# Four attention heads one projection tile earlier, and two residual scalings in other places

## The reference

```python
for l in range(DEPTH):                      # DEPTH = 2
    h = rmsnorm_2(x, attn_norm[l])
    proj = jnp.einsum('bsd,de->bse', h, w_in[l])          # 1024 -> 3072
    sb_q, sb_k, sb_v, df_q, df_k, df_v = jnp.split(proj, splits, axis=-1)
    sb_out = stick_breaking_attention(...)                # 8 heads of 64
    dq, dk = rope(df_q ...), rope(df_k ...)               # 4 heads, two maps of 64 each
    df_heads = differential_attention(dq, dk, dvv, lam)   # softmax(map 0) - lam * softmax(map 1)
    df_out = rmsnorm_2(df_heads, subln_norm[l]) * (1.0 - lambda_init)
    x = x + jnp.einsum('bse,ed->bsd', mixed, w_o[l])
    h = rmsnorm_2(x, mlp_norm[l])
    u = jnp.square(jax.nn.relu(h @ w_ff1[l]))
    x = x + u @ w_ff2[l]
```

## Time and profile before

| | us |
|---|---|
| median of 3 runs | 1552.63 (1552.49 to 1553.12) |
| profiled execution | 1552.31 |
| its span | 1550.6 |
| TensorE busy | 1528.4 |
| VectorE busy | 1060.4 |
| ScalarE busy | 820.0 |

### The profile page before, as it was taken

How to read it: one execution, slowest core, us unless ns; L and a number is a source line. 1 busy time by engine, 2 the same in 40 slices (tenths; PEclk the granted TensorE clock), 3 DMA queues, 4 the chain that set the end, 5 groups by cost and what they waited for, 6 DMA issues and landing times.

```text
span 1550.6 us, 23427 instructions
## 1 busy us (share of the span) xinstructions
PE 1528.4 (99%) x8755; PEld 1292.1 (83%) x8755; DVE 1060.4 (68%) x1774; ACT 820.0 (53%) x1399; POOL 181.4 (12%) x146
## 2 busy tenths in 40 slices
PE   8999999999999999999999999999999999999998
PEld 7777888777788778898989888888788898989886
DVE  6886557566876876875858555775885885848653
ACT  5556533555655864645445335664874645545332
POOL 4001222032000213010100011000223010100001
PEclk9999999999999999999999999999999999999999
DMA  5211232322221113332332323212112233232331
GB/s 179 74 56 55 82 95 96 109 96 82 82 80 58 55 55 96 109 104 87 103 99 98 109 82 109 82 55 82 55 55 82 91 101 109 83 108 90 100 109 55
DMA packets 127300, 135.83 MB, mean 88 GB/s; under 512 B 2458, under 2 KB 120804, under 8 KB 127204
## 3 DMA queue, kind: packets, MB, share of 16 engines
q1 hardware_dynamic: 126048, 133.18, 26.9%
q0 software_dynamic: 288, 1.05, 0.2%
q10 hardware_dynamic: 868, 0.31, 0.1%
HBM read 132.43 MB, written 2.10 MB: 87 GB/s over the span
## 4 chain that ended last, share of the span: by engine, by line
PE 89%; DVE 3%; issue 3%; ACT 2%; POOL 1%; DVEq 0%; POOLq 0%; ACTq 0%
PE U L1942 19%; PE U L1944 19%; PE U L1943 19%; PE Z L2250 3%; PE Z L2251 3%; PE Z L2249 3%; PE U L1987 2%; PE U L1989 2%; PE U L1988 2%; PE U L2251 1%; PE U L2249 1%; PE U L2250 1%; PE Z L2124 1%; PE O L2176 1%; PE Z L2139 1%
## 5 line engine op out<-in xcount | busy, mean ns | idle before, releaser
L1942 PE MATMUL U<-MH,WL 128*128 128x512 f32 x848 | 337.2, 398 | 1.9 <-DVE tb L1610 1.7
L1944 PE MATMUL U<-MH,WH 128*128 128x512 f32 x848 | 331.1, 390 | 0.0
L1943 PE MATMUL U<-ML,WH 128*128 128x512 f32 x848 | 330.8, 390 | 0.0
L1132 DVE TENSOR_TENSOR WL<-raw,WH 128x1024 fp32r<-128x1024 f32 x181 | 234.6, 1296 | 81.6 <-ACT WH L643 71.9
L1942 PE MATMUL U<-XH,WL 128*128 128x512 f32 x592 | 237.3, 401 | 2.2 <-DVE WL L1455 1.1
L1944 PE MATMUL U<-XH,WH 128*128 128x512 f32 x592 | 231.4, 391 | 0.0
L1943 PE MATMUL U<-XL,WH 128*128 128x512 f32 x592 | 231.1, 390 | 0.0
L643 ACT ACTIVATE WH<-raw 128x1024 fp32r<-128x1024 f32 x197 | 205.7, 1048 | 19.1 <-PE Z L2251 16.7
L1942 PEld LDWEIGHTS U<-MH,WL 128*128 128x128 f32 x848 | 159.4, 188 | 43.2 <-issue 8.4
L1944 PEld LDWEIGHTS U<-MH,WH 128*128 128x128 f32 x848 | 159.3, 188 | 33.8
L1943 PEld LDWEIGHTS U<-ML,WH 128*128 128x128 f32 x848 | 159.6, 188 | 31.6 <-issue 0.7
(11 more groups left out here) (303 smaller groups left out, 3059.6 us busy)
## 6 DMA issues: line engine op xcount, KB each, us to landing
raw<-in_w_ff SPq DMA_DIRECT2D x64, 1024.0 KB, 5.4
raw<-in_w_in SPq DMA_DIRECT2D x24, 1024.0 KB, 5.1
raw<-in_attn_w_in SPq DMA_DIRECT2D x9, 1024.0 KB, 5.2
raw<-in_pool_w_in SPq DMA_DIRECT2D x8, 1024.0 KB, 5.5
raw<-in_w_o SPq DMA_DIRECT2D x8, 1024.0 KB, 5.1
raw<-in_attn_w_out SPq DMA_DIRECT2D x4, 1024.0 KB, 5.1
raw<-in_pool_w_out SPq DMA_DIRECT2D x4, 1024.0 KB, 5.2
xin<-in_x SPq DMA_DIRECT2D x2, 1024.0 KB, 6.5
```

Of the source, the lines that this page charges most:

```text
L1132: v.tensor_tensor(w_slot(WL, t, shape), src, w_slot(WH, t, shape).bitcast(F32), ALU.subtract).then_inc(lo_done, 1)
L1942: mm(o, wl, xh, start=first, stop=False, **kw)
L1943: mm(o, wh, xl, start=False, stop=False, **kw)
L1944: return mm(o, wh, xh, start=False, stop=last, **kw)
```

## The change

The head's first tile becomes 4+3d instead of 5+3d, and with it every step of a differential head comes one tile earlier in both layers. The scores of heads 0 and 2 then stand two tiles behind their query tile (tiles 4 and 10, queries in 2 and 8) instead of three. The third residual scaling of layer 0 moves from tile 4 to tile 6, the fourth from tile 7 to tile 9. VectorE's ordinary tile gains the branch for `df_f`, because head 3's last transpose now falls in tile 17 instead of 18. No instruction is added or removed on any engine.

```diff
--- before.py
+++ after.py
@@ -95,7 +95,7 @@
             return step
 
         for d in range(4):
-            first = 4 * (5 + 3 * d)
+            first = 4 * (4 + 3 * d)
             for i, when in enumerate((0, 2, 2)):
                 at(first + when, op="df_qk", d=d, i=i)
             for i in range(3):
@@ -1409,8 +1409,8 @@
                 if value_tile:
                     take(s, 0, l)
                     conv(s["t"] + 2)
-                if l == 0 and at in (2, 3, 4):
-                    residual((0, 2, 4)[at - 2])
+                if l == 0 and at in (2, 3):
+                    residual((0, 2)[at - 2])
                 for st in df_t:
                     if st["i"] == 1 and not (value_tile and before["kind"] in ("dfk", "dfq")):
                         df_evict(st)
@@ -1419,8 +1419,10 @@
                     df_norm(st, l)
                 for st in steps_of(s, "sb_o"):
                     sb_low(st)
-                if l == 0 and at == 7:
-                    residual(6)
+                for st in steps_of(s, "df_f"):
+                    df_low(st, l)
+                if l == 0 and at in (6, 9):
+                    residual(4 if at == 6 else 6)
 
             df_mix = {l: {i + 1: st["d"] for i, x in enumerate(plan["layer", l]) for st in x["steps"] if st["op"] == "df_qk" and st["i"] == 2}
                       for l in range(DEPTH)}
```

## The result

| | before | after |
|---|---|---|
| median, us | 1552.57 (1552.49 to 1553.12, 4 runs) | 1573.53 (1572.20 to 1573.96, 4 runs) |
| profiled execution, us | 1552.31 | 1573.96 |
| span, us | 1550.6 | 1572.2 |
| TensorE busy, us | 1528.4 | 1538.3 |
| granted clock, mean | 0.999 | 0.994 |

The ratio is 1.0134, interval 1.0122 to 1.0146: 21.0 us slower, where 13.8 were forecast and the range ended at 1571.5. The direction and every forecast wait of 0.7 us or more came. The prediction failed on one step, TensorE's clock.

What follows compares the result with a forecast made beforehand. TensorE, busy 1528.4 of 1550.6 us, was taken as the bound, so new waits add time. Terms of 6.75 (layer 0) and 7.05 (layer 1) give 13.8 on 1552.3: 1566.1, median 1566.4, range 1561.5 to 1571.5.

Steps and rivals of the forecast that it cites:

- Scores of head 0: Tile 4: TensorE waits for VectorE's add of tile 2's rotated query, +1.9 us in layer 0, +2.2 in layer 1.
- Head 0's combination, tile 6: VectorE's combination in tile 5 delays its value take, so TensorE starts tile 6 late, +0.7 us in each layer.
- Tiles 10 to 12: Late normalization and value takes put tile 12 at S+15.4 (S: start of head's second score round), +2.4 us each layer.
- Head 1's turns: Tile 9: ScalarE evicts turn 0 behind shifts waiting for the previous rotation; turn 1 late, +2.2 us in each layer.
- Head 2 and 3: Tiles 13 to 17: nothing added, with 0.3 us a layer as other bound, for the last transpose in tile 17.
- First stick-breaking turns: Tiles 18 to 20: VectorE's second softplus step starts 0.9 us sooner; -0.45 us each layer, bounds 0 and -0.86.
- Residual scalings: Two of 1.41 us move from tiles 4 and 7 to 6 and 9; counted as nothing, at most 1.4 once.
- The clock: Fall to half clock behind tile 4's 3.6 us wait in layer 0: 1.6 us lost, or 5.8; not in the sum.
- 1: Rival: late handoff at tile 9 costs less than counted, 4.4 us gone, 1562.0 us; chance 0.13.
- 2: Rival: delays spread, three or four more waits of 0.3 to 1.4 us in two layers, 1569 to 1570; chance 0.12.
- 3: Rival: the clock falls behind the first gap, 1568 to 1572 us; chance 0.07.
- 4 and 5: Rivals: everything new is ready in time, 1550.9 or 1549.2 us; or the change has nil effect, 1552.6; together 0.05.

Runs made afterwards that it cites:

- Experiment 4: Experiment 3's kernel with head 0's scores two parts later in tile 4: 1563.19 us, ratio 1.0071.
- Experiment 9: Changed kernel with head 0 alone one tile early, heads 1 to 3 as before, fourth residual scaling in tile 7: 1563.14 us, ratio 1.0062.
- Experiment 3: Experiment 2's kernel, with VectorE taking the first result of value tiles 5 and 11 ahead of the combination: 1567.57 us, ratio 1.0090.
- Experiment 2: Changed kernel with ScalarE's eviction of head 1's turn 0 in tile 9 put ahead of the four shifts: 1573.53 us, ratio 1.0137.
- Experiment 11: Kernel before, with layer 0's residual scalings in tiles 3, 4, 7 and 13 instead of 2, 3, 4 and 7: 1551.56 us, ratio 0.9990.
- experiment 1: Changed kernel with 54 extra matmuls, results unread, filling TensorE's idle places ahead of its waits: 1567.62 us, ratio 1.0097.
- experiment 6: Changed kernel with the edits of Experiment 2, Experiment 3, Experiment 4 and experiment 5 together (four repairs): 1558.63 us, ratio 1.0037.
- experiment 7: Kernel before, with head 1's turn 0 in tile 10 evicted behind the shifts, a lone wait in each layer: 1561.34 us, ratio 1.0052.
- experiment 8: Kernel before, with VectorE's low part of head 3 in tile 18 behind the second softplus step: 1553.12 us, ratio 1.0003.
- experiment 5: Experiment 2's kernel, with VectorE's copy of head 1's turn 1 ahead of the rotation's sine product and add: 1570.63 us, ratio 1.0115.

## Why the prediction was wrong, point by point

**Scores of head 0:** right, 1.93 and 2.21 by starts, against 1.9 and 2.2. Experiments 4 and 9 tie them to this step.

**Head 0's combination, tile 6:** right, 0.7 shown in each layer. **Tiles 10 to 12:** right within 0.3, though the small waits within tile 11 that were part of the sum do not show: in layer 1 from S (1041.98) to tile 12 (1057.15) it is 15.17, against S+15.4. Experiment 3 removes both with one take ahead of the combination, so the named order was the cause.

**Head 1's turns:** right, 2.2 each, eviction behind shifts. Experiment 2 showed that the forecast chain was only half of it: the same late rotation holds VectorE's copy, which would have cost the same 2.2. The step was right for one of two equal reasons.

**Head 2 and 3:** nearly right. I put nothing for the last transposes and named 0.3 a layer as the bound; head 2's cost 0.35 in layer 1. I had looked for it at head 3.

**First stick-breaking turns:** right in mechanism; the wait of 0.86 is 0.24 (forecast about 0.4). **Residual scalings:** right at nothing. Experiment 11 shows that it is the scaling of tile 2 that costs, 1.5 us, and the change leaves it in its place.

**The clock: the step that failed.** I wrote "If the clock fell for 3.2 us behind it, half of these are lost, 1.6 us", allowed this for one gap, the one of 3.6 us, and gave it a chance of 0.07. In the sum itself the clock stands at nothing. The size for one fall came out right, 1.7 measured against 1.6, but by luck: the 3.2 us of the earlier trace rows end where that stretch was cut off, at 1550. In that trace the clock is at half in the whole of 1548 to 1550 and does not come back before the span ends, so the row doesn't show how long a fall lasts. The count was wrong, and the chance too low. Four waits had a fall behind them, those of 3.6, 2.2, 2.2 and 1.8 us, and the term is 6.8 us by the records and 5.9 by experiment 1. With it the sum for the profiled execution is 1566.1 + 6.8 = 1572.9, against 1573.96; for the median, experiment 1's term gives 1566.4 + 5.9 = 1572.3, against 1573.53. I took the 1.72 us wait in a run of clock 0.999 as a sign that waits are harmless, though I was forecasting six waits of 1.9 us and more, all longer than any that the row covered. That row is good evidence up to 1.72, and experiments 4, 6, 7 and 8 confirm it there; it says nothing of 2.2. The rule that I quoted beside it, from the Trainium skill, page "TensorE: Matmul & The Clock Gate", section "HAM oscillation — how this bites in real kernels", says that the price is paid again at each gap. The runs agree in part: in the profiled execution after, four of the six new waits paid it, and over all runs the table above has the share. I priced it once.

**The rivals.** 1 fell: the late handoff cost its full 2.2. 2 fell, for the waits were nearly all the forecast ones; of its places only head 2's last transpose in tile 14 came, with 0.35. 3 was the right mechanism and would have ended at 1572, because it too had one fall. 4 and 5 fell with the direction.

## What to carry to other kernels

Where a change leaves a busy TensorE standing, price each new wait twice: its length, and the chance of a fall of the clock behind it if it is longer than the longest wait that the profile before shows without one. Count the falls place by place, and let the range reach to a fall behind every such wait. When a wait comes from an order on another engine, list everything that stands behind the late instruction: moving one customer ahead only uncovers the next, and here the tile of distance between producer and consumer was worth 5.6 us more than four repairs.

## What the runs showed of the hardware that was not expected

- A stretch at half clock came to 3.4 us in 18 of 22 falls and to twice that, 6.8, in the other four, all four behind the 3.6 us wait. In those four the clock had fallen while TensorE still stood; in the other 18 TensorE had started again before it fell.
- The fall need not begin at once. Behind tile 12's wait the matmuls ran at full pace from 1057.15 and slowed at 1058.62; in experiment 5 the clock was down before TensorE had started again, at 392.83:

```profile
390.00:392.00 2.00, 0.00 (x0) 0.00 (x0) 2.00 (x3) 0.44 (x1) 0.00 (x0) 0.86 0.02 7
```

- The 54 matmuls of experiment 1, whose results nobody reads, made the kernel 5.9 us faster: they stood where TensorE was idle, and the clock no longer fell.
- A wait as shown is some 0.16 us shorter than the delay by starts, since a 512-wide matmul is shown 0.39 long and the next can start after 0.227.
